# A three-block attention and MLP kernel: the low part of five weight blocks by GpSimd subtraction, and the third block's key, value and query rows interleaved

## The chip, the cores and the metric

The kernel runs on one core of a Trainium2 chip. The metric is the time of one execution on the device in microseconds (us), lower is better. PE is TensorE, ACT is ScalarE, DVE is VectorE, POOL is GpSimd and SP is SyncE, which only issues copies here.

## The reference

Two layers of one kind (l = 0 and 1 in the code) are followed by one of another kind (called 2). Between layers stands a layer norm, and ahead of the third block an RMS norm as well. All is float32.

```python
for l in range(DEPTH):                                   # DEPTH = 2
    proj = jnp.einsum('bld,de->ble', h, w_in[l])
    a, g, zc, q, k, v, za, qi, ki, wi = jnp.split(proj, IN_SPLITS, axis=-1)
    ...                                                  # convolution branch, sparse attention branch
    y = jnp.einsum('ble,ed->bld', jnp.concatenate([y_conv, y_attn], axis=-1), w_out[l])
    h = layer_norm(DEEPNORM_ALPHA * h + y, post_ln_g[l], post_ln_b[l])
x = h[:, N_META:L]
...
h = rmsnorm(x, norm_gain)                                # the third block
z = jnp.einsum('bsd,de->bse', h, w_in)
q, k, v, gate_a, u_in, v_in, gate_b, g_merge = jnp.split(z, IN_SPLITS_2, axis=-1)
q = axial_rope(rmsnorm(q, q_gain), row_ang, col_ang)
k = axial_rope(rmsnorm(k, k_gain), row_ang, col_ang)
```

The width is 1024, and there are 512 positions and 16 meta positions: row tile 0 has 16 rows, tiles 1 to 4 have 128 each.

## The kernel before

**Products in three passes.** PE multiplies with operands in a reduced format (fp32r). Each operand is split in a high part and the remainder, the low part, and a product is high x high, high x low and low x high (`PASSES`). `xhi` and `xlo` hold the turned rows of x: ACT writes `xhi` out of PSUM (`x_hi`, L807), DVE subtracts and writes `xlo` (`x_lo`, L1958). PE's products wait for `x_lo`.

**The weight stream.** Weights come in blocks of 128x2048 (1 MB) through a ring of four buffers. The list `USES` gives PE's order of products and `BLOCKS` the last use of each block. SP loads block n into `raw[n % 4]` when the last use of block n - 4 is done (L555). ACT then writes the high part `whi` (L631) and the negated high part `wlo`, which lies over the raw block (L632), both in `split_hi`. POOL then issues a copy that adds the weights from memory onto `wlo` (`split_lo`, L1050), so that raw - high is left. PE waits in `weights(n)` for that copy. `SPLIT_AT` says after which product a block is split; `next_blocks(use)` does it on ACT and on POOL. Only the first two blocks of the program get their low part from DVE.

**The borders.** Every engine runs its own list in order; nothing is scheduled at run time. At the end of a layer come, for the last row tiles, the two halves (convolution, attention) of the output products (`output_half`, L1428), then on DVE for each tile t `residual` (L1911, L1919), `aggregate` (L1924) and `post_norm` (L1934: h<-h,meanvar,post_ln_g; L1938: h<-h,rstd,post_ln_b), between the two on POOL `ln_deviation` (L1059 and L1062, which write `rstd`). PE turns the rows (`turn_rows`, L1412). Ahead of the third block ACT forms a sum of squares (`squares`, L817), POOL `input_deviation` and DVE `second_input` (L1950: h_normed<-h,rstd,norm_gain), before the rows are turned. The first products of layer 1 are those of a and g, over tiles 0 to 2 first and over tiles 3 and 4 after. The third block begins with kv (1 block, 256 columns) for its four row tiles, then q (2 blocks, 512 columns) for four, each product in bank A or B by turns (`rows`, L1279); a bank is free when ACT has taken its rows (L925, L928). SP issues `load_mix`, which waits for the last `post_norm`, right after q's second block.

## Time and profile before

| | us |
|---|---|
| median of 3 runs | 1060.81 |
| runs | 1059.41 to 1061.35 |
| profiled execution | 1061.86 |
| its span | 1060.1 |
| PE busy | 999.9 (94%) |
| DVE busy | 653.6 (62%) |
| ACT busy | 582.7 (55%) |
| POOL busy | 197.7 (19%) |

The span is the profiled execution from its first to its last instruction; 1.8 us lie around it. All times of rows are counted from the start of the span. The border between layers 0 and 1 lies at about 332 to 372 us, the one between layer 1 and the third block at 658 to 726 us. PE's matmuls are pipelined, so their busy time is not time at PE's peak; where PE stands still shows in the idle time ahead of an instruction. A releaser is inferred from semaphores, and where one instruction waits for several things the last by the profile is named.

### The profile page before, as it was taken

Reading aid. Unit: us, or ns where it says so; the run is one execution under the profiler, and the core shown is the slowest. Engines: PE = TensorE matmul, PEld = TensorE weight load, DVE = VectorE, ACT = ScalarE, POOL = GpSimd, SP = SyncE. Lnnn points to the kernel's source line nnn. Section 1 sums busy time; section 2 is a strip of 40 time slices with the busy share of each in tenths; the row PEclk is TensorE's granted clock in tenths of the full one; section 3 lists DMA queues with packets and bytes.
Section 4 is the critical chain, followed back from the end, with each engine's and each line's share of the span. In section 5 each row is a group of like instructions: output and inputs, shape, how many; then the busy total and the mean of one; then the engine's idle time right before and its main releaser. Section 6 shows DMA issues by size and latency. Waiting matters only on the chain.

```text
span 1060.1 us, 16512 instructions
## 1 busy us (share of the span) xinstructions
PE 999.9 (94%) x6452; PEld 845.2 (80%) x6452; DVE 653.6 (62%) x1423; ACT 582.7 (55%) x944; POOL 197.7 (19%) x238
## 2 busy tenths in 40 slices
PE   6999999898999899999999799789999899999997
PEld 6998988875577898898888577678888778887885
DVE  3899999866573489899977556626521433332522
ACT  6585882557444558587255734634555555554321
POOL 0000771013121100076101212223200000000001
PEclk9999999998999999999989999979999999999999
DMA  7776874734203777487464521765777545456651
GB/s 287 182 181 178 209 175 118 187 92 120 40 1 98 181 170 177 121 192 181 113 164 100 153 60 40 202 158 147 183 181 207 130 104 125 115 134 144 163 155 80
DMA packets 23820, 152.35 MB, mean 144 GB/s; under 512 B 2864, under 2 KB 3376, under 8 KB 6848
## 3 DMA queue, kind: packets, MB, share of 16 engines
q0 software_dynamic: 9648, 68.75, 34.8%
q1 hardware_dynamic: 14096, 82.55, 21.3%
q8 instruction: 52, 0.85, 0.3%
q14 instruction: 24, 0.20, 0.1%
HBM read 149.20 MB, written 2.10 MB: 143 GB/s over the span
## 4 chain that ended last, share of the span: by engine, by line
PE 61%; DVE 20%; ACT 9%; issue 7%; POOL 1%; DMA 1%; POOLq 0%; SPq 0%; DVEq 0%; ACTq 0%
PE psum_B L1246 15%; PE psum_A L1246 9%; PE psum_B L1279 7%; PE psum_A L1279 7%; DVE conv_acc L1723 6%; DVE score L1782 5%; PE psum_A L1428 5%; DVE top L1773 5%; PE psum_B L1428 2%; PE psum_A L1639 2%; PE psum_B L1382 2%; PE psum_B L1639 2%; ACT w_hi L631 2%; ACT w_lo L632 2%; PE psum_A L1357 1%
## 5 line engine op out<-in xcount | busy, mean ns | idle before, releaser
L1723 DVE SCALAR_TENSOR_TENSOR conv_acc<-u,vec,conv_acc 128x528 f32<-128x528 f32 (+1 forms) x240 | 172.1, 755 | 3.2
L1050 POOL DMA_DIRECT2D w_lo<-in_weights x67 | 59.4, 887 | 595.0 <-ACT w_lo L632 568.8
L1246 PE MATMUL psum_B<-x_hi,w_hi 128*128 128x264 f32 (+3 forms) x480 | 134.8, 321 | 5.2 <-DVE mlp_lo L2176 3.6
L631 ACT ACTIVATE w_hi<-w_raw 128x2048 fp32r<-128x2048 f32 (+2 forms) x85 | 129.3, 1521 | 15.0 <-DMA w_raw<-in_weights 14.5
L1246 PE MATMUL psum_B<-x_lo,w_hi 128*128 128x264 f32 (+3 forms) x480 | 132.5, 317 | 0.0
L1246 PE MATMUL psum_B<-x_hi,w_lo 128*128 128x264 f32 (+3 forms) x480 | 132.1, 316 | 0.0
L1246 PE MATMUL psum_A<-x_hi,w_hi 128*128 128x264 f32 (+2 forms) x528 | 127.3, 295 | 2.2 <-DVE za L1870 1.2
L632 ACT ACTIVATE w_lo<-w_raw 128x2048 fp32r<-128x2048 f32 (+2 forms) x85 | 128.6, 1513 | 0.0
L1246 PE MATMUL psum_A<-x_lo,w_hi 128*128 128x264 f32 (+2 forms) x528 | 124.6, 290 | 0.0
L1246 PE MATMUL psum_A<-x_hi,w_lo 128*128 128x264 f32 (+2 forms) x528 | 124.5, 290 | 0.0
L1246 PEld LDWEIGHTS psum_A<-x_hi,w_hi 128*128 128x128 f32 x528 | 89.4, 192 | 6.5 <-issue 3.3
L1246 PEld LDWEIGHTS psum_B<-x_hi,w_hi 128*128 128x128 f32 (+1 forms) x480 | 81.4, 185 | 13.7 <-issue 7.6
L1246 PEld LDWEIGHTS psum_A<-x_lo,w_hi 128*128 128x128 f32 x528 | 89.5, 192 | 0.8
L1246 PEld LDWEIGHTS psum_A<-x_hi,w_lo 128*128 128x128 f32 x528 | 89.3, 192 | 0.7
L1246 PEld LDWEIGHTS psum_B<-x_hi,w_lo 128*128 128x128 f32 (+1 forms) x480 | 81.4, 185 | 6.2
L1246 PEld LDWEIGHTS psum_B<-x_lo,w_hi 128*128 128x128 f32 (+1 forms) x480 | 81.4, 185 | 5.6
L1279 PE MATMUL psum_A<-w_hi,x_hi 128*128 128x512 f32 (+1 forms) x144 | 56.7, 394 | 4.9 <-DMA w_lo<-in_weights 2.6
L1279 PE MATMUL psum_B<-w_hi,x_hi 128*128 128x512 f32 (+1 forms) x144 | 56.5, 392 | 4.1 <-issue 4.1
L1782 DVE MATCH_REPLACE8 score<-top,score 128x528 f32<-128x528 f32 (+2 forms) x102 | 56.1, 561 | 0.0
L1279 PE MATMUL psum_B<-w_hi,x_lo 128*128 128x512 f32 (+1 forms) x144 | 55.9, 388 | 0.0
L1279 PE MATMUL psum_B<-w_lo,x_hi 128*128 128x512 f32 (+1 forms) x144 | 55.9, 388 | 0.0
L1279 PE MATMUL psum_A<-w_hi,x_lo 128*128 128x512 f32 (+1 forms) x144 | 55.7, 387 | 0.0
(349 smaller groups left out, 2121.9 us busy)
## 6 DMA issues: line engine op xcount, KB each, us to landing
w_raw<-in_weights SPq DMA_DIRECT2D x67, 1024.0 KB, 5.2
w_lo<-in_weights POOLq DMA_DIRECT2D x65, 1024.0 KB, 8.4
x_first<-in_x_t SPq DMA_DIRECT2D x4, 528.0 KB, 6.9
h<-in_x SPq DMA_DIRECT2D x1, 2048.0 KB, 10.8
out<-h SPq DMA_DIRECT2D x4, 512.0 KB, 2.6
post_ln_g<-in_post_ln_g SPq DMA_DIRECT2D x2, 512.0 KB, 6.9
post_ln_b<-in_post_ln_b SPq DMA_DIRECT2D x2, 512.0 KB, 7.9
w_raw<-in_weights SPq DMA_DIRECT2D x2, 288.0 KB, 5.3
```

The source lines that it names most:

```text
L631: act.activation(whi[n % RING][:, a:b], raw[n % RING][:, a:b], ACT.Copy)
L632: got = act.activation(wlo[n % RING][:, a:b], raw[n % RING][:, a:b], ACT.Copy, scale=-1.0)
L1050: pool.dma_start(wlo[n % RING][:, 0:width], io["weights"][n, :, 0:width], accum_op=ALU.add) \
L1246: mm = pe.matmul(ps[0:cols, i, 0:b - a], w[wp][:, kt, at:at + cols], x[xp][:, kt, a:b], start=(kt == 0 and wp + xp == 0), stop=(kt == KD - ...
L1279: mm = pe.matmul(ps[:, 0, 0:width], act_parts[xp][:, kt, c0:c0 + P], w[wp][:, kk, at:at + width], start=(kt == 0 and wp + xp == 0), stop=( ...
L1357: pe.transpose(main[:, 0, (j - 1) * P:(j - 1) * P + n], src[0:n, START[j]:END[j]], ident[0:n, 0:n])
L1382: mm = pe.matmul(ps[s:s + HD, 0, hd // 2 * P:hd // 2 * P + n], keys, probs, start=(j == 0), stop=(j == t))
L1428: mm = pe.matmul(ps, x[xp][:, kt, START[t]:START[t] + P], w[wp][:, kk, 0:DC], start=(kt == 0 and wp + xp == 0), stop=(kt == KD - 1 and wp ...
L1639: mm = pe.matmul(ps[:, 0, :], w[wp][:, kt, d % 4 * P:d % 4 * P + P], parts[xp][:, kt, :], start=(kt == 0 and wp + xp == 0), stop=(kt == CT ...
L1723: got = dve.scalar_tensor_tensor(dst, src, w, dst, ALU.mult, ALU.add)
L1773: dve.max(top8[:, t - 1, :], vals).then_inc(topk_max.mark((l, r, t)), 1)
L1782: dve.match_replace(vals, top8[:, t - 1, :], vals, MARK).then_inc(topk_marked.mark((l, r, t)), 1)
```

## The change

`LO_BY_POOL` names five blocks: a and g of layer 1, kv and the two of q. For these ACT writes the high part in two halves of 1024 columns and no negated copy, POOL subtracts high from raw for each half and writes `wlo` (`subtract_hi`), and PE waits for the second half's signal. No copy adds weights for them. In the third block PE's order becomes kv 0, kv 1, q 0, kv 2, kv 3, q 1, q 2, q 3 (`KV_AND_Q`), with the turn of tile 3 after kv 1 and that of tile 4 after q 0. In layer 1 the attention half of output tile (0, 4) goes ahead of that of (1, 3), DVE's residuals follow, and ACT's splits and squares are placed anew. SP issues `load_mix` one block later.

```diff
@@ -83,6 +83,9 @@
+KV_AND_Q = (("kv", 0), ("kv", 1), ("q", 0), ("kv", 2), ("kv", 3), ("q", 1), ("q", 2), ("q", 3))
 def weight_stream():
@@ -111,8 +114,11 @@
             uses.extend((l, "wo", n, t) for t in tiles if (n, t) < (1, 3) and t < 4)
-        uses.extend([(l, "wo", 0, 4, "conv"), (l, "wo", 1, 4, "conv"), (l, "wo", 1, 3, "conv"), (l, "wo", 1, 3),
-                     (l, "wo", 0, 4), (l, "wo", 1, 4)])
+        uses.extend([(l, "wo", 0, 4, "conv"), (l, "wo", 1, 4, "conv"), (l, "wo", 1, 3, "conv")])
+        if l < DEPTH - 1:
+            uses.extend([(l, "wo", 1, 3), (l, "wo", 0, 4), (l, "wo", 1, 4)])
+        else:
+            uses.extend([(l, "wo", 0, 4), (l, "wo", 1, 3), (l, "wo", 1, 4)])
@@ -143,8 +149,9 @@
     blocks.append(((l, "kv", 0), BLOCK, (l, "kv", 3)))
-    uses.extend((l, "kv", t) for t in range(4))
-    halves(l, "q", range(4))
+    for half in range(2):
+        blocks.append(((l, "q", half), BLOCK, (l, "q", 3)))
+    uses.extend((l, *row) for row in KV_AND_Q)
     for name in ("vin", "u", "gb"):
@@ -161,6 +168,8 @@
 NUMBER = {key: n for n, (key, _, _) in enumerate(BLOCKS)}
+LO_BY_POOL = {NUMBER[key] for key in ((1, "a", 0), (1, "g", 0), (2, "kv", 0), (2, "q", 0), (2, "q", 1))}
@@ -609,7 +619,7 @@
                 load_weights(n)
-                if key == (2, "q", 1):
+                if key == (2, "vin", 0):
                     load_mix()
@@ -627,6 +637,12 @@
                     act.activation(whi[n][:, a:b], raw[n][:, a:b], ACT.Copy).then_inc(hi_made.mark(("w", n)), 1)
+                    return
+                if n in LO_BY_POOL:
+                    for half in range(2):
+                        a, b = half * BLOCK // 2, (half + 1) * BLOCK // 2
+                        act.activation(whi[n % RING][:, a:b], raw[n % RING][:, a:b], ACT.Copy) \
+                            .then_inc(hi_made.mark(("w", n, half)), 1)
                     return
@@ -909,13 +925,10 @@
                     x_hi(l, 1)
+                    next_blocks((l, "wo", 0, 4))
                     x_hi(l, 2)
+                    next_blocks((l, "wo", 1, 3))
                     squares(3, square)
-                    next_blocks((l, "wo", 1, 3))
-                    x_hi(l, 3)
-                    squares(4, square)
-                    next_blocks((l, "wo", 1, 4))
-                    x_hi(l, 4)
@@ -933,7 +946,6 @@
                     act.activation(sgb[t][:, :], ps[:, 0, :], ACT.Silu).then_inc(act_took.mark(use), 1)
-                next_blocks(use)
@@ -996,12 +1008,20 @@
-            for name in ("kv", "q"):
-                for t in range(4):
-                    take_rows(name, t)
+            for name, t in KV_AND_Q:
+                take_rows(name, t)
+                if (name, t) == ("kv", 1):
+                    x_hi(DEPTH - 1, 3)
+                    squares(4, square)
+                elif (name, t) == ("q", 0):
+                    x_hi(DEPTH - 1, 4)
+                    split_hi(NUMBER[(2, "vin", 0)])
+                elif name == "q":
+                    next_blocks((2, "q", t))
             for name in ("vin", "u", "gb"):
                 for t in range(4):
                     take_rows(name, t)
+                    next_blocks((2, name, t))
                     if name == "u":
@@ -1043,6 +1063,13 @@
         def _(pool):
+            def subtract_hi(n, half):
+                a, b = half * BLOCK // 2, (half + 1) * BLOCK // 2
+                pool.wait_ge(hi_made.sem, hi_made.at(("w", n, half)))
+                pool.tensor_tensor(wlo[n % RING][:, a:b], raw[n % RING][:, a:b], whi[n % RING][:, a:b].bitcast(F32),
+                                   ALU.subtract).then_inc(pool_lo.mark((n, half)), 1)
             def split_lo(n):
@@ -1154,15 +1181,27 @@
-                next_blocks((l, "wo", 1, 4, "conv"))
-                ln_deviation((l, "post", 3), 3, P)
-                if l == DEPTH - 1:
+                if l < DEPTH - 1:
+                    a_in, g_in = NUMBER[(1, "a", 0)], NUMBER[(1, "g", 0)]
+                    subtract_hi(a_in, 0)
+                    subtract_hi(a_in, 1)
+                    ln_deviation((l, "post", 3), 3, P)
+                    subtract_hi(g_in, 0)
+                    subtract_hi(g_in, 1)
+                    ln_deviation((l, "post", 4), 4, P)
+                    next_blocks((l, "wo", 1, 4))
+                else:
+                    kv_in, q_in = NUMBER[(2, "kv", 0)], NUMBER[(2, "q", 0)]
+                    subtract_hi(kv_in, 0)
+                    subtract_hi(kv_in, 1)
+                    subtract_hi(q_in, 0)
+                    ln_deviation((l, "post", 3), 3, P)
+                    subtract_hi(q_in, 1)
                     input_deviation(3)
-                next_blocks((l, "wo", 1, 3))
-                ln_deviation((l, "post", 4), 4, P)
-                if l == DEPTH - 1:
+                    subtract_hi(q_in + 1, 0)
+                    ln_deviation((l, "post", 4), 4, P)
+                    subtract_hi(q_in + 1, 1)
                     input_deviation(4)
-                next_blocks((l, "wo", 1, 4))
@@ -1174,11 +1213,11 @@
+            split_lo(NUMBER[(2, "vin", 0)])
             for t in range(4):
-                next_blocks((2, "kv", t))
                 unit_scale("k", t)
+            next_blocks((2, "q", 1))
             for t in range(4):
-                next_blocks((2, "q", t))
                 unit_scale("q", t)
@@ -1223,8 +1262,11 @@
                     pe.wait_ge(first_lo.sem, first_lo.at(n))
+                elif n in LO_BY_POOL:
+                    pe.wait_ge(pool_lo.sem, pool_lo.at((n, 1)))
                 elif n:
-                    pe.wait_ge(weights_lo[n % RING], 16 * (n // RING + (n % RING >= BY_DVE)))
+                    added = [m for m in range(n % RING, n + 1, RING) if m >= BY_DVE and m not in LO_BY_POOL]
+                    pe.wait_ge(weights_lo[n % RING], 16 * len(added))
                 return whi[n % RING], wlo[n % RING]
@@ -1548,13 +1590,17 @@
                 output_conv(l, 1)
-                if l == DEPTH - 1:
-                    turn_rows(l, 1)
-                output_rows(l, 1, 3, "A", 0)
                 if l < DEPTH - 1:
+                    output_rows(l, 1, 3, "A", 0)
                     turn_rows(l, 0)
                     turn_rows(l, 1)
-                output_attn(l, 0)
+                    output_attn(l, 0)
+                else:
+                    turn_rows(l, 1)
+                    ps = claim((l, "wo", 1, 3), "A", (0,))[:, 0, :]
+                    output_half(l, 1, 0, 3, ps).then_inc(psum_full.mark((l, "wo", 1, 3, "conv")), 1)
+                    output_attn(l, 0)
+                    output_half(l, 1, 1, 3, ps).then_inc(psum_full.mark((l, "wo", 1, 3)), 1)
                 turn_rows(l, 2)
@@ -1640,13 +1686,16 @@
-            for t in range(4):
-                x_ready(1, t + 1)
-                rows((2, "kv", t), NUMBER[(2, "kv", 0)], x, META + P * t, 1, 2 * P, 0, KD)
-                if t < 2:
-                    turn_rows(1, t + 3)
-            for t in range(4):
-                rows((2, "q", t), NUMBER[(2, "q", 0)], x, META + P * t, 2)
+            for name, t in KV_AND_Q:
+                if name == "kv":
+                    x_ready(1, t + 1)
+                    rows((2, "kv", t), NUMBER[(2, "kv", 0)], x, META + P * t, 1, 2 * P, 0, KD)
+                    if t == 1:
+                        turn_rows(1, 3)
+                else:
+                    rows((2, "q", t), NUMBER[(2, "q", 0)], x, META + P * t, 2)
+                    if t == 0:
+                        turn_rows(1, 4)
             for name in ("vin", "u", "gb"):
@@ -2048,13 +2097,13 @@
                     x_lo(l, 1)
+                    residual(l, 0, 4)
                     residual(l, 1, 3)
                     aggregate(l, 3)
                     post_norm(l, 3)
-                    residual(l, 0, 4)
                     x_lo(l, 2)
+                    residual(l, 1, 4)
                     second_input(3)
-                    residual(l, 1, 4)
                     aggregate(l, 4)
                     post_norm(l, 4)
                     x_lo(l, 3)
```

The order of POOL's instructions at the border to the third block, before (w_lo_59 is kv's block, w_lo_60 and w_lo_57 are q's, w_lo_58 is vin's first):

```order
163 L1070 TENSOR_TENSOR x_lo<-y_part_125,x_hi 128x4x128
164 L1050 DMA w_lo_59<-in_weights 128x2048
165 L1059 TENSOR_SCALAR var_eps<-meanvar 128x1
166 L1062 TENSOR_TENSOR rstd<-var_eps,minus_half 128x1
167 L1059 TENSOR_SCALAR var_eps<-prob_sums 128x1
168 L1062 TENSOR_TENSOR rstd<-var_eps,minus_half 128x1
169 L1050 DMA w_lo_60<-in_weights 128x2048
170 L1059 TENSOR_SCALAR var_eps<-meanvar 128x1
171 L1062 TENSOR_TENSOR rstd<-var_eps,minus_half 128x1
```

The same place on POOL now (L1070 is the subtraction in `subtract_hi`):

```order
164 L1070 TENSOR_TENSOR w_lo_59<-w_raw_55,w_hi_51 128x1024 x2
165 L1070 TENSOR_TENSOR w_lo_60<-w_raw_56,w_hi_52 128x1024
166 L1086 TENSOR_SCALAR var_eps<-meanvar 128x1
167 L1089 TENSOR_TENSOR rstd<-var_eps,minus_half 128x1
168 L1070 TENSOR_TENSOR w_lo_60<-w_raw_56,w_hi_52 128x1024
169 L1086 TENSOR_SCALAR var_eps<-prob_sums 128x1
170 L1089 TENSOR_TENSOR rstd<-var_eps,minus_half 128x1
171 L1070 TENSOR_TENSOR w_lo_57<-w_raw_53,w_hi_49 128x1024
172 L1086 TENSOR_SCALAR var_eps<-meanvar 128x1
173 L1089 TENSOR_TENSOR rstd<-var_eps,minus_half 128x1
174 L1070 TENSOR_TENSOR w_lo_57<-w_raw_53,w_hi_49 128x1024
```

Subtractions now stand ahead of and between the deviations of tiles 3 and 4 (var_eps, rstd), where issues of copies stood.

POOL at the border between layers 0 and 1 before, with the waits (w_lo_58 is a's block, w_lo_59 g's):

```order
86 L1050 DMA w_lo_58<-in_weights 128x2048 [waits weights_minus]
87 L1059 TENSOR_SCALAR var_eps<-meanvar 128x1 [waits stats_made]
88 L1062 TENSOR_TENSOR rstd<-var_eps,minus_half 128x1 [waits pool_step]
89 L1050 DMA w_lo_59<-in_weights 128x2048 [waits weights_minus]
90 L1059 TENSOR_SCALAR var_eps<-meanvar 128x1 [waits stats_made]
```

And now:

```order
86 L1070 TENSOR_TENSOR w_lo_58<-w_raw_54,w_hi_50 128x1024 [waits hi_made] x2
87 L1086 TENSOR_SCALAR var_eps<-meanvar 128x1 [waits stats_made]
88 L1089 TENSOR_TENSOR rstd<-var_eps,minus_half 128x1 [waits pool_step]
89 L1070 TENSOR_TENSOR w_lo_59<-w_raw_55,w_hi_51 128x1024 [waits hi_made] x2
90 L1086 TENSOR_SCALAR var_eps<-meanvar 128x1 [waits stats_made]
```

The two halves of each block take the place of one issue; DVE's order at this border is what it was.

ACT at the border to the third block now, from the first split on (w_hi_51 is kv's block, w_hi_52 and w_hi_49 q's, w_hi_50 vin's):

```order
510 L644 ACTIVATE w_hi_51<-w_raw_55 128x1024 [waits raw_loaded2]
511 L644 ACTIVATE w_hi_51<-w_raw_55 128x1024
512 L823 ACTIVATE x_hi<-psum_D 128x8x128 [waits psum_full]
513 L644 ACTIVATE w_hi_52<-w_raw_56 128x1024 [waits raw_loaded3]
514 L644 ACTIVATE w_hi_52<-w_raw_56 128x1024
515 L823 ACTIVATE x_hi<-psum_C 128x8x128 [waits psum_full]
516 L644 ACTIVATE w_hi_49<-w_raw_53 128x1024 [waits raw_loaded0]
517 L644 ACTIVATE w_hi_49<-w_raw_53 128x1024
518 L833 ACTIVATE square,prob_sums<-h 128x1024 [waits exp_made,normed]
519 L941 ACTIVATE qk_row_173<-psum_A 128x128 [waits psum_full]
```

Both of q's blocks are split ahead of the square of tile 3; before, the first followed that square, and the second that of tile 4.

## Rows read from the trace of the kernel before

**Rows 1.** Chain that ended last, border to third block: start, length, what.
```profile
688.92 5.04 PE psum_A L1279 x24
693.97 4.10 issue
698.07 5.46 PE psum_B L1279 x24
...
720.28 5.56 PE psum_B L1279 x24
```

**Rows 2.** Timeline of PE there: start, length, instruction, idle before and releaser.
```profile
674.21 0.40 PE L1428 MATMUL psum_B<-w_lo,x_hi 128*128 128x512 f32 x1
677.18 0.36 PE L1279 MATMUL psum_A<-w_hi,x_hi 128*128 128x256 f32 x1 [2.58 <-DMA w_lo<-in_weights]
...
680.11 1.03 PE L1412 MATMUL psum_D<-ident,h_normed 128*128 128x128 f32 x8
680.90 0.36 PE L1279 MATMUL psum_B<-w_hi,x_hi 128*128 128x256 f32 x1
```

**Rows 3.** Busy time by window: PE, PEld, DVE, ACT, POOL, clock, DMA, GB/s.
```profile
690.00:710.00 20.00, 15.90 (x74) 14.49 (x74) 3.89 (x19) 5.62 (x10) 4.42 (x9) 0.75 0.77 186
```

**Rows 4.** Timeline of PE at the border of layers 0 and 1.
```profile
349.74 0.36 PE L1246 MATMUL psum_A<-x_hi,w_hi 128*128 128x264 f32 x1 [1.05 <-DVE x_lo L1958]
...
359.97 0.36 PE L1246 MATMUL psum_D<-x_hi,w_hi 128*128 128x264 f32 x1 [2.40 <-DVE x_lo L1958]
```

**Rows 5.** Landing of copies issued at 347.3 (w_lo), 665.4 and 683.7 (w_raw).
```profile
DMA to landing us min/median/max: 12.6/12.6/12.6
...
DMA to landing us min/median/max: 6.0/6.0/6.0
...
DMA to landing us min/median/max: 10.2/10.2/10.2
```

**Rows 6.** The page's part 6: issues, KB each, median us to landing.
```profile
w_raw<-in_weights SPq DMA_DIRECT2D x67, 1024.0 KB, 5.2
w_lo<-in_weights POOLq DMA_DIRECT2D x65, 1024.0 KB, 8.4
```

**Rows 7.** Timeline of ACT: high parts at both borders.
```profile
343.21 1.91 ACT L631 ACTIVATE w_hi<-w_raw 128x2048 fp32r<-128x2048 f32 x1
...
662.21 1.92 ACT L631 ACTIVATE w_hi<-w_raw 128x2048 fp32r<-128x2048 f32 x1 [2.01 <-DMA w_raw<-in_weights]
...
693.93 1.91 ACT L631 ACTIVATE w_hi<-w_raw 128x2048 fp32r<-128x2048 f32 x1 [5.11 <-DMA w_raw<-in_weights]
```

**Rows 8.** POOL's subtractions by shape (count, busy us, mean ns); then min/median/max ns.
```profile
L1070 POOL TENSOR_TENSOR x_lo<-y_part,x_hi 128x64 fp32r<-128x64 f32 x2 | 0.6, 317 | 6.7 <-ACT x_hi L777 6.7
...
L1070 POOL TENSOR_TENSOR x_lo<-y_part,x_hi x18: 314/1282/1597, 224.5 to 660.3; 128x512 fp32r<-128x512 f32 x16, 128x64 fp32r<-128x64 f32 x2
```

**Rows 9.** Timeline of POOL beside DVE, and durations of DVE's L1950.
```profile
660.27 1.60 POOL L1070 TENSOR_TENSOR x_lo<-y_part,x_hi 128x512 fp32r<-128x512 f32 x1 [11.82 <-ACT x_hi L777]
...
669.96 1.27 POOL L1059 TENSOR_SCALAR var_eps<-meanvar 128x1 f32<-128x1 f32 x1 [2.77 <-DVE meanvar L1924]
...
674.54 0.19 POOL L1059 TENSOR_SCALAR var_eps<-prob_sums 128x1 f32<-128x1 f32 x1 [2.66 <-ACT square L817]
...
L1950 DVE SCALAR_TENSOR_TENSOR h_normed<-h,rstd,norm_gain x4: 1276/1282/2312, 659.4 to 684.5; 128x1024 f32<-128x1024 f32 x4
```

**Rows 10.** Timeline of DVE at both borders.
```profile
344.49 1.27 DVE L1934 SCALAR_TENSOR_TENSOR h<-h,meanvar,post_ln_g 128x1024 f32<-128x1024 f32 x1
345.80 1.28 DVE L1938 SCALAR_TENSOR_TENSOR h<-h,rstd,post_ln_b 128x1024 f32<-128x1024 f32 x1
...
348.33 1.21 DVE L1958 TENSOR_TENSOR x_lo<-psum_C,x_hi 128x1024 fp32r<-128x1024 f32 x1
...
669.90 1.28 DVE L1934 SCALAR_TENSOR_TENSOR h<-h,meanvar,post_ln_g 128x1024 f32<-128x1024 f32 x1
...
674.51 1.21 DVE L1958 TENSOR_TENSOR x_lo<-psum_C,x_hi 128x1024 fp32r<-128x1024 f32 x1
```

More of the change, by code:

```diff
@@ L501, in build @@
         first_lo = signal("first_lo")
+        pool_lo = signal("pool_lo")
         psum_full = signal("psum_full")
```

## The prediction

> **What bounds the kernel now.** I read the page first: TensorE (PE) is busy 94% of the span, so a change pays only where PE stands still or runs at a low clock. Next I read the chain of waits around the two places that the diff touches. At the border between the second and third block the chain shows the kv product of tile 2 taking 5.04 us, then 4.10 us of idle, then that of tile 3 taking 5.46 us [rows 1]. PE also waited 2.58 us for the low part of kv; the product of kv 0 then took 2.93 us, from 677.18 to the turn at 680.11 [rows 2]. From 690 to 710 the granted clock is 0.75 while PE is busy 15.90 of 20 us [rows 3]. So this border loses at least 6.7 us in idle time (2.58 + 4.10) and 4.6 us in clock (5.04 + 5.46 less 2 x 2.93). At the border between the first and second block PE loses only 1.05 us (for x_lo of tile 2) and 2.40 us [rows 4]. The latter is put down to x_lo, but the g block's low part, issued at 347.3, took 12.6 us to land [rows 5], which is 359.83, 0.14 us before PE goes on. That product reads tiles 0 to 2 alone, so the transfer held it.
>
> **Low part by subtraction.** Removed for five blocks: ACT's second 1.9 us pass, a GpSimd issue of 0.9 us and an accumulating transfer of 8.4 us median [rows 6]. Added: per block two 128x1024 subtractions. 128x512 took 1.28 us (the median) and 128x64 0.32 us [rows 8]; the line through them gives 2.38 us for 1024 columns (0.32 + 960 x 2.15 ns), and doubling the first 2.56. No row shows this form, so the bounds are 2.3 and 2.6 and I take 2.4, the line's value. ACT's half pass is 0.95 us, half of 1.90 [rows 7]. So a low part is ready 0.95 + 4.8 = 5.8 us after ACT starts, where before it took 3.6 + 8.4 us or more.
>
> The Trainium skill (GPSIMD Engine Reference, 3.1 Elementwise) gives 4497 ns for a fp32 subtraction-like operation of 2048 columns; as an estimate that is 2.25 us for 1024 and would make the gain some 0.6 us larger. No row of this trace has that width.
>
> **What the subtraction does to VectorE.** The gain is not free. When GpSimd's 128x512 subtraction began waiting at 660.27 it took 1.60 instead of 1.28, and the VectorE operation h_normed<-h,gain that came behind it took 2.31 us, where the others of its kind took 1.28 [rows 9]. The other way round var_eps took 1.27 us at 669.96, all of it beside h<-h,ln_g, but 0.19 us beside x_lo<-psum,x_hi [rows 9, 10]. I read: a VectorE operation with two SBUF inputs and a GpSimd operation exclude each other, and whichever has begun keeps the other out until about its end; one with a PSUM input is free. A 2.4 us subtraction can then hold back a post_norm (two such operations) by 2.2 to 2.4 us each time, and post_norm stands ahead of x_lo, which PE needs.
>
> The Trainium skill (SBUF — State Buffer, section SBUF: two separate sides) calls this "an exclusive lock, not a bandwidth split", kept for the whole instruction. It speaks against this change; the rows show it for 1.3 us operations alone. With that rule the sum is the one below; if long operations shared instead, it would be the third rival.
>
> **First border, step by step.** a's low part is ready at 335.8 + 0.95 + 4.8 = 341.6 instead of 348.8, but PE waits for x_lo of tile 2 (VectorE 348.33 + 1.21 [rows 10]), so nothing is gained. g: ACT's first half ends at 343.21 + 0.95 = 344.2 [rows 7], GpSimd runs 344.3 to 346.7. VectorE wants h<-h,ln_g at 344.49 [rows 10]: it gets 346.5 to 347.8. GpSimd's second half has waited and goes before VectorE's dependent second operation: 347.8 to 350.2. VectorE's h<-h,rstd,ln_b then starts at 350.0 instead of 345.80, so x_lo of tile 2 starts at 348.33 + 4.2, and PE begins the a product at 353.9 instead of 349.74: 4.2 us lost. PE has stood 5.4 us by then. After 4.10 us of standing the product took 5.46 instead of 2.9; I put 1.5 us on the clock here, between 0 and 2.5. The 2.40 us wait for g's transfer goes. What is late next there is x_lo of tiles 3 and 4, 2.3 us behind the turn of tile 4, covered by the g product of 2.9 us. Sum: 4.2 + 1.5 - 2.4 = **3.3 us lost**. If VectorE gets h<-h,ln_g in first (0.2 us decides), one subtraction less stands in the way: about 2.2 us lost, less a clock that stays high: near 0. Ends: 4.5 lost, 2.4 won.
>
> The second layer between the borders has the same order and waits as before, so it moves as one; PE's two spells of low clock in it may fall otherwise, worth 1.5 us either way.
>
> **Second border.** PE's queue: attention half of (0,4) ahead of that of (1,3), which lets q's second block load 2.8 us earlier; kv 0, kv 1, turn 3, q 0, turn 4, kv 2, kv 3, q 1 to 3. SP loads vin's first block right when its buffer is free (674.6) and not behind load_mix, which waits for the last post_norm; that load started at 683.7 and landed 10.2 us later [rows 5], and ACT stood 5.11 us for it at 693.93 [rows 7] with kv 1's rows, which PE waited for, behind it. This is the 4.10 us. Times of before, carried through the new queues:
> - kv: raw at 662.2 [rows 7], both low halves at 668.1. PE starts kv 0 right after the last output product, which began at 674.21 [rows 2]: 674.4 instead of 677.18.
> - q's first block: issued at 665.41, landed after 6.0 us before [rows 5] with the kv transfer beside it; alone 5.2 [rows 6], so 670.6. ACT's first half 671.6, GpSimd 671.6 to 674.0. ln_deviation of tile 3, for which statistics are there at 672.6, is queued behind it. h<-h,ln_g 673.9 to 675.1; ln_deviation 675.1 to 675.9; then GpSimd goes straight into the next subtraction, 675.9 to 678.3, and h<-h,rstd,ln_b waits again: 678.2 to 679.5. x_lo of tile 2 is ready at 680.7, so kv 1 starts at 680.9, where it started before [rows 2]. The 2.8 us won by kv 0 are lost, and PE has stood 3.5 us, so I let kv 1 take 5.2 us at low clock: 686.1, turn 3: 687.0.
> - q 0, two halves of 2.8: 687.0 to 692.8. q's second block is subtracted at 681.6 to 684.0 and 687.4 to 689.8, in time for the second half at 690.
> - The second subtraction holds the second operation of tile 4's post_norm until 689.7; square, input_deviation and second_input follow to 694.3. Turn 4 begins at 694.5 (PE stands 1.7), kv 2 at 695.3, kv 3 at 698.2, q 1 at 701.2, each q row 5.56 us: q 3 ends at 717.8 instead of 725.8 [rows 1]. **8.0 us won.** The waits for ACT are gone, since kv 1's rows are taken at 686.4 and vin's split stands behind tile 4.
> - vin's second block is split after q 1 (707.4 to 711.0), its transfer lands 8.4 us after (719.5 to 721); PE wants it at 720.6. I put 0.2 us; 1.2 at the far end.
>
> Ends for this border: VectorE favoured in each contest 8 to 9 won; subtraction of 2.6 us 7.3; raw landings as before (6.0 and 7.9) 7.2. From q 3 on all orders are as before.
>
> **Sum.** 3.3 - 8.0 + 0.2 = -4.5 us. The profiled execution took 1061.86 us (span 1060.1 and 1.8 around it), so 1057.4 in its terms; it stands 1.05 above the median of the three runs, 1060.81, from which I forecast **1056.3 us**. A comparison of this kernel can tell about 0.2%, 2.1 us, from no change.
>
> **Rivals.**
> 1. VectorE gets in ahead of GpSimd at the borders (0.18). For it: at the first border 0.2 us decides, and after a GpSimd operation VectorE has been the one waiting. Against: at 660.7 GpSimd, having waited, went before VectorE's next. First border 0, second 8.2 to 9: 1052.2.
> 2. Slower: the 128x1024 subtraction takes much longer than its line says (0.12). GpSimd's queue is then the bound: four subtractions stand in the chain of the second border and two at the first, and every ln_deviation is behind one. Each microsecond more costs about 4.2 and up to 2 us. At 3.15 us a half nothing is won; at 3.6 us it is 1063.5. Against it: 16 operations of 512 columns took 1.28 us in the middle and 1.60 at most [rows 8], also while ACT and the DMA engines work. Raw blocks landing 5 us late, as vin's did [rows 5], would have the same effect on a smaller scale.
> 3. The long subtraction does not hold VectorE back (0.05): first border 2.4 won; at the second PE never stands and q 3 ends at 674.4 + 4 x 2.93 + 4 x 5.56 + 1.6 for the turns and 1.2 for short waits, 711.2, so 14.6 won: 1044.0. Against: rows 9.
> 4. The gain is as reckoned at one border and lost to clock or a late vin transfer (0.17): within 2.1 us of before, 1059.5.
> The forecast as reckoned, 1054 to 1058.5, has 0.48.
>
> **Range and chances.** 1050.5 to 1060.5 holds the forecast, most of rival 1 and much of rival 4. Faster by over 0.2%: 0.48 + 0.18 + 0.05 = 0.71; within: 0.17; slower: 0.12.
>
> **What would show it.** In the profile after: GpSimd's 128x1024 subtractions at 2.4 us; h<-h,ln_g and h<-h,rstd,ln_b at 344 to 351 and 673 to 680 taking up to 3.5 us instead of 1.28, or starting late; PE's a product near 353.9 and no wait for g; kv 0 straight after the output products, kv 1 no earlier than before; no ACT wait for w_raw at 694; q 3 ending about 4.5 us earlier by the profile's clock, since the first border's loss is carried along. It would be wrong if the first border gains, or if kv 1 starts before 680.9 plus the first border's shift.

## The result, and the profile after

The changed kernel is slower: 1064.93 us median of 4 runs beside 1060.11 for the kernel before on the same chip, ratio 1.0048 (95% interval 1.0030 to 1.0067). A second comparison, below, gave 1.0034 (1.0017 to 1.0051). I had forecast 1056.3 us. The profiled execution has a span of 1063.0 us (1060.1 before); PE, DVE and POOL are busy 1000.8, 663.9 and 218.1 us.

**First border.** Timelines of POOL and then of DVE in the changed kernel: start, length, instruction (L1070 is the subtraction).

```profile
338.65 4.74 POOL L1070 TENSOR_TENSOR w_lo<-w_raw,w_hi 128x1024 fp32r<-128x1024 f32 x2 [1.96 <-ACT w_hi L644]
346.10 5.70 POOL L1070 TENSOR_TENSOR w_lo<-w_raw,w_hi 128x1024 fp32r<-128x1024 f32 x2 [1.10 <-ACT w_hi L644]
...
346.25 3.32 DVE L1983 SCALAR_TENSOR_TENSOR h<-h,meanvar,post_ln_g 128x1024 f32<-128x1024 f32 x1
349.61 3.27 DVE L1987 SCALAR_TENSOR_TENSOR h<-h,rstd,post_ln_b 128x1024 f32<-128x1024 f32 x1
```

The two DVE operations took 1.27 and 1.28 us before [rows 10]. They are stretched by 2.0 us each, beside g's two subtractions. PE's timeline and the chain show what follows (before: [rows 4]):

```profile
355.54 0.56 PE L1288 MATMUL psum_A<-x_hi,w_hi 128*128 128x264 f32 x1 [5.08 <-DVE x_lo L2007]
...
355.54 5.62 PE psum_A L1288 x24
361.15 0.88 PE psum_D L1454 x8
362.04 2.90 PE psum_B L1288 x24
```

PE stands 5.08 us, not 1.05, and the first product after it takes 5.62 us, the next 2.90 (it took 3.15 us before). The granted clock is 0.66 from 354 to 364.

**Second border.** The timelines of POOL and PE:

```profile
677.12 2.42 POOL L1070 TENSOR_TENSOR w_lo<-w_raw,w_hi 128x1024 fp32r<-128x1024 f32 x1 [3.35 <-ACT w_hi L644]
...
686.71 0.55 PE L1321 MATMUL psum_B<-w_hi,x_hi 128*128 128x256 f32 x1 [3.60 <-DVE h L1960]
...
699.53 1.06 PE L1454 MATMUL psum_C<-ident,h_normed 128*128 128x128 f32 x8 [0.88 <-DVE h_normed L1999]
```

So far it went as the steps said. The chain behind that had no place in them. It runs from kv 2 to vin's first row tile:

```profile
700.60 2.85 PE psum_B L1321 x24
703.44 2.85 PE psum_A L1321 x24
706.32 10.50 DMA w_raw<-in_weights
716.84 1.92 ACT w_hi L647
718.75 1.81 ACT w_lo L648
720.57 0.43 issue
721.00 8.82 DMA w_lo<-in_weights
729.82 0.04 issue
729.87 4.52 PE psum_A L1321 x12
```

kv 3 ends at 706.3 and frees the buffer for vin's second block; its copy takes 10.5 us, the split 3.7, the accumulating transfer 8.8. PE has done the q rows and half of vin's first row tile by then, stands 4.13 us, and does the other half at a low clock, 4.52 us instead of 2.78 (half of a row's 5.56); the granted clock is 0.72 from 729 to 735. PE's timeline, the first matmul of the late half:

```profile
729.87 0.79 PE L1321 MATMUL psum_A<-w_hi,x_hi 128*128 128x512 f32 x1 [4.13 <-DMA w_lo<-in_weights]
```

**How stretches are compared.** Single times can't be set side by side, because the executions differ before the first border already: the layer's last y_part starts at 332.21 in the profile of before and 333.97 in that of after. I therefore measure each border from that layer's own last y_part. These are the four rows for the changed kernel (DVE's y_part, u and y_part, then ACT's first v_normed):

```profile
333.97 0.69 DVE L1937 SCALAR_TENSOR_TENSOR y_part<-psum_B,za 128x512 f32<-128x512 f32 x1 [5.80 <-PE psum_B L1424]
376.45 0.71 DVE L1755 SCALAR_TENSOR_TENSOR u<-shifted,u 128x528 f32<-128x528 f32 x1 [8.32 <-ACT shifted L691]
664.50 0.69 DVE L1937 SCALAR_TENSOR_TENSOR y_part<-psum_B,za 128x512 f32<-128x512 f32 x1 [5.80 <-PE psum_B L1424]
734.43 0.60 ACT L944 ACTIVATE v_normed<-psum_A 128x512 f32<-128x512 f32 x1 [9.54 <-PE psum_A L1321]
```

Their differences are border 1 (42.5), the layer between, and border 2 (69.9). "To a" is from y_part to PE's first a product, "vin to end" from that v_normed to the end of the span. The same instructions give, in every profile of this study:

| kernel | to a | border 1 | between | border 2 | vin to end |
|---|---|---|---|---|---|
| before, four profiles | 17.5 all | 38.6, 37.9, 38.0, 38.6 | 288.0, 287.9, 288.3, 288.1 | 72.6, 68.7, 69.5, 72.6 | 328.6 all |
| changed, two profiles | 21.6 both | 42.5, 42.5 | 288.0, 288.1 | 69.9, 71.5 | 328.6, 329.0 |
| first border undone, two | 17.5 both | 38.9, 39.0 | 287.9, 288.1 | 69.8, 69.8 | 328.6 both |
| first border alone | 21.6 | 42.6 | 288.1 | 72.5 | 328.6 |
| vin subtracted | 21.6 | 42.6 | 288.1 | 64.1 | 328.6 |
| vin's first block only | 21.6 | 42.8 | 288.0 | 64.1 | 328.6 |
| vin's second block only | 21.6 | 42.5 | 288.1 | 64.0 | 328.5 |
| pieces of 512 columns | 19.4 | 39.4 | 288.0 | 69.4 | 328.6 |
| undone, vin subtracted | 17.5 | 42.0 | 288.3 | 64.1 | 328.6 |
| 512, vin subtracted | 19.4 | 39.4 | 286.3 | 62.3 | 328.7 |
| 256, vin subtracted, two | 18.3 both | 36.8, 38.3 | 286.8, 288.0 | 64.8, 63.5 | 328.6, 328.7 |
| 512, vin subtracted, plain order | 19.4 | 39.4 | 286.7 | 70.8 | 328.6 |

The last column says that nothing comes back later (one profile of the changed kernel is 0.4 us longer there): what a border wins or loses stays.

### The profile page after: what moved, and what is told of

Read it like the earlier page. It is cut to its first block, busy times and chain, and to the rows that moved or that the text cites. A ratio compares the mean times of both kernels' runs of the same rounds, so it can differ in the third digit from the quotient of the medians.

```text
span 1063.0 us, 16517 instructions
## 1 busy us (share of the span) xinstructions
PE 1000.8 (94%) x6452; PEld 846.8 (80%) x6452; DVE 663.9 (62%) x1423; ACT 574.3 (54%) x944; POOL 218.1 (21%) x243
## 4 chain that ended last, share of the span: by engine, by line
PE 58%; DVE 21%; ACT 9%; issue 7%; DMA 3%; POOL 1%; POOLq 0%; DVEq 0%; SPq 0%; ACTq 0%
PE psum_B L1288 15%; PE psum_A L1288 9%; DVE conv_acc L1772 6%; PE psum_B L1321 5%; PE psum_A L1321 5%; DVE score L1831 5%; DVE top L1822 5%; PE psum_A L1470 5%; PE psum_B L1470 2%; PE psum_A L1685 2%; DMA w_raw<-in_weights 2%; PE psum_B L1685 2%; PE psum_B L1424 2%; ACT w_hi L647 2%; ACT w_lo L648 2%
## 5 line engine op out<-in xcount | busy, mean ns | idle before, releaser
L1077 POOL DMA_DIRECT2D w_lo<-in_weights x62 | 54.8, 884 | 579.5 <-ACT w_lo L648 553.3
L647 ACT ACTIVATE w_hi<-w_raw 128x2048 fp32r<-128x2048 f32 (+2 forms) x80 | 119.8, 1497 | 10.0 <-DMA w_raw<-in_weights 9.4
L648 ACT ACTIVATE w_lo<-w_raw 128x2048 fp32r<-128x2048 f32 (+2 forms) x80 | 119.1, 1489 | 0.0
## 6 DMA issues: line engine op xcount, KB each, us to landing
w_raw<-in_weights SPq DMA_DIRECT2D x2, 288.0 KB, 5.4
```

The source lines that it names most:

```text
L647: act.activation(whi[n % RING][:, a:b], raw[n % RING][:, a:b], ACT.Copy)
L648: got = act.activation(wlo[n % RING][:, a:b], raw[n % RING][:, a:b], ACT.Copy, scale=-1.0)
L1077: pool.dma_start(wlo[n % RING][:, 0:width], io["weights"][n, :, 0:width], accum_op=ALU.add) \
```

## Experiments

**Which border loses.** Two kernels take the change apart. In the first, a and g get their low parts by transfer again:

```diff
-LO_BY_POOL = {NUMBER[key] for key in ((1, "a", 0), (1, "g", 0), (2, "kv", 0), (2, "q", 0), (2, "q", 1))}
+LO_BY_POOL = {NUMBER[key] for key in ((2, "kv", 0), (2, "q", 0), (2, "q", 1))}
...
                 if l < DEPTH - 1:
-                    a_in, g_in = NUMBER[(1, "a", 0)], NUMBER[(1, "g", 0)]
-                    subtract_hi(a_in, 0)
-                    subtract_hi(a_in, 1)
+                    next_blocks((l, "wo", 1, 4, "conv"))
                     ln_deviation((l, "post", 3), 3, P)
-                    subtract_hi(g_in, 0)
-                    subtract_hi(g_in, 1)
+                    next_blocks((l, "wo", 1, 3))
```

> The changed kernel with the border between the two layers as before: the low parts of the a and g blocks come again by the accumulating transfer. Theory A (the loss has two places): in the profile after, the first border ends 3.9 us later than before (374.6 against 369.0, less the 1.8 us by which that execution lay behind already), and the second wins only 2.7. With the first undone the time falls by about 4 us from the changed kernel, to 0.996 to 0.998 of the kernel before. Theory B (the first border's loss is of that one execution, and the rest of the change costs time): it stays at 1.003 to 1.005 of the kernel before. Theory C (both borders lose): 1.001 to 1.003.

The second is the kernel before with only these two blocks subtracted (the same edit the other way round, on the kernel before).

> The kernel before with only the low parts of a and g at the border between the layers by GpSimd subtraction; the third block is as before. Theory A: 3.9 us slower, 1.003 to 1.005; the two DVE passes of the post-norm at 346 to 353 take 3.3 us each instead of 1.3, and the first product after the border runs at the lower clock. Theory B: 0.999 to 1.001. The two halves of the change should add up: this ratio and that of the kernel with the first border undone should make that of the whole change when multiplied.

Measured: 1.0006 (0.9990 to 1.0023) and 1.0038 (1.0017 to 1.0060). Their product is 1.0044, so the halves add up to the whole. The first border's loss is real and is the whole loss: border 1 takes 42.6 us with it and 38.9 without. But my own theory missed 0.996 to 0.998 for the first: by its stretches the second half of the change wins 2.8 us against the first profile of before, and no such gain is in its time. That was open until the profiles of before were repeated (below).

**Why vin is late.** Both vin blocks are subtracted too:

```diff
-LO_BY_POOL = {..., (2, "q", 0), (2, "q", 1))}
+LO_BY_POOL = {..., (2, "q", 0), (2, "q", 1), (2, "vin", 0), (2, "vin", 1))}
...
+            def low_part(n):
+                if n in LO_BY_POOL:
+                    subtract_hi(n, 0)
+                    subtract_hi(n, 1)
+                else:
+                    split_lo(n)
+
             def next_blocks(use):
                 for n in SPLIT_AT.get(use, []):
-                    split_lo(n)
+                    low_part(n)
...
-            split_lo(NUMBER[(2, "vin", 0)])
+            low_part(NUMBER[(2, "vin", 0)])
```

> The changed kernel, with both vin blocks' low parts by GpSimd subtraction too. Theory A says that the second border gives back 6 us at vin, since its second block's copy lands 10.5 us after its issue beside the first block's accumulating transfer, and its own accumulating transfer takes 8.8 more. Both transfers are gone here: TensorE's idle 6.5 us between the halves of vin's row tile 0 goes, and the time falls by 5 to 7 us from the changed kernel, to 0.998 to 0.9995. Rival: the copy lands as late and the ScalarE rows of q delay the split, so that TensorE waits as long: 1.004 to 1.005. A second rival: the subtractions hold GpSimd from the scales of k and q and VectorE's passes on them, so that part comes back later in the third block: 1.001 to 1.003.

Measured 0.9970 (0.9954 to 0.9986), which is lower than I expected; border 2 takes 64.1 us instead of 69.9. Its chain has nothing but PE left, from kv 3 through the q rows to vin 0:

```profile
703.97 2.84 PE psum_A L1328 x24
706.81 5.55 PE psum_B L1328 x24
712.36 5.56 PE psum_A L1328 x24
717.92 5.56 PE psum_B L1328 x24
723.48 5.56 PE psum_A L1328 x24
```

Two more kernels subtract one vin block each (only the set in the first two lines differs). Both have one profile each and no ratio of their own, so the stretches speak for them.

> The changed kernel with only vin's first block by subtraction; its second keeps the accumulating transfer. If the second block's copy is late because it runs beside the first block's accumulating transfer, the copy now lands about 5 us after kv 3's end instead of 10.5 (in the kernel with both subtracted it did), the split starts right after q 1, its transfer lands near 725, and TensorE waits at most 1 us in vin's row tile 0: second stretch 64 to 65.5 us instead of 69.9. Rival (the copy is late for another reason, and the accumulating transfer of the second block is what costs): the copy lands after 9 to 10 us, second stretch 68 to 70 us.

> The changed kernel with only vin's second block by subtraction; the first keeps the accumulating transfer. The second block's copy should land late again, 10 to 11 us after kv 3's end, since the transfer is beside it; the two hi halves and subtractions take 6 us from there, so that the low part is there about 723, 3 us before TensorE wants it: no wait, second stretch 64 to 64.6 us, as with both subtracted. If GpSimd's scales of k and q come in between, up to 66.

Landing of vin's second raw block, issued at kv 3's end, in the changed kernel, with vin's first block subtracted, and with only the second:

```profile
DMA to landing us min/median/max: 10.5/10.5/10.5
...
DMA to landing us min/median/max: 5.0/5.0/5.0
...
DMA to landing us min/median/max: 10.3/10.3/10.3
```

So the copy takes twice as long when the first block's accumulating transfer, issued 0.7 us before it, is under way. Issued 0.9 us ahead of such a transfer, a copy landed after 6.0 us [rows 5]. Border 2 takes 64.1 and 64.0 us: taking away either the collision or the last transfer removes the whole wait. It needs both a late copy and 8.8 us of transfer behind it.

**What DVE waits for.** Every subtraction is cut into pieces of 512 columns, with the semaphore on the last:

```diff
-                pool.tensor_tensor(wlo[n % RING][:, a:b], raw[n % RING][:, a:b], whi[n % RING][:, a:b].bitcast(F32),
-                                   ALU.subtract).then_inc(pool_lo.mark((n, half)), 1)
+                for c in range(a, b, 512):
+                    got = pool.tensor_tensor(wlo[n % RING][:, c:c + 512], raw[n % RING][:, c:c + 512],
+                                             whi[n % RING][:, c:c + 512].bitcast(F32), ALU.subtract)
+                got.then_inc(pool_lo.mark((n, half)), 1)
```

> The changed kernel with every subtraction in pieces of 512 columns rather than 1024. If a DVE pass with two SBUF inputs waits for the GpSimd operation that is under way (an exclusive lock held for one operation), its wait falls from up to 2.4 us to up to 1.2: the two post-norm passes of the first border take 2.0 to 2.8 us rather than 3.3, and the time falls by 1 to 2 us, to 1.002 to 1.004 of the kernel before. If the slowdown is one of shared bandwidth, the piece's size changes nothing: passes of 3.3 us, 1.004 to 1.005. If the lock is won by GpSimd again at each piece, DVE waits longer than now: over 1.005.

Measured 0.9986 (0.9969 to 1.0002): 6.6 and 5.1 us under the changed kernel by its two ratios, where its stretches say 3.6 (3.1 at border 1, 0.5 at border 2) and I had expected 1 to 2. The passes of 2.2 us are those of the first hypothesis; the time lies below all three. DVE's two post-norm operations of the first border, with pieces of 512, and then of 256 columns in a later kernel (vin subtracted there as well):

```profile
343.91 2.22 DVE L1985 SCALAR_TENSOR_TENSOR h<-h,meanvar,post_ln_g 128x1024 f32<-128x1024 f32 x1
346.17 2.20 DVE L1989 SCALAR_TENSOR_TENSOR h<-h,rstd,post_ln_b 128x1024 f32<-128x1024 f32 x1
...
346.56 1.68 DVE L1992 SCALAR_TENSOR_TENSOR h<-h,meanvar,post_ln_g 128x1024 f32<-128x1024 f32 x1
348.27 1.64 DVE L1996 SCALAR_TENSOR_TENSOR h<-h,rstd,post_ln_b 128x1024 f32<-128x1024 f32 x1
```

And the subtractions' durations (ns, min/median/max) with 1024, 512 and 256 columns (all ten of the first kernel, those of the first border in the others):

```profile
L1070 POOL TENSOR_TENSOR w_lo<-w_raw,w_hi x10: 2379/2398/3346, 338.7 to 692.3; 128x1024 fp32r<-128x1024 f32 x10
...
L1071 POOL TENSOR_TENSOR w_lo<-w_raw,w_hi x8: 1256/1290/2273, 336.2 to 349.5; 128x512 fp32r<-128x512 f32 x8
...
L1071 POOL TENSOR_TENSOR w_lo<-w_raw,w_hi x16: 718/730/1730, 338.9 to 353.2; 128x256 fp32r<-128x256 f32 x16
```

These DVE operations, with two SBUF inputs, are stretched by 2.0, 0.9 and 0.4 us where the GpSimd operation takes 2.4, 1.3 and 0.7: each time by one GpSimd operation less 0.3 to 0.4 us. PE's a product moves by just twice that (4.0, 1.9 and 0.8 us). The first border also pays less clock: the a product took 5.62 us with 1024 columns and 4.44 with 512, where PE stands 2.9 us ahead of it instead of 5.1.

> As the kernel with pieces of 512 and vin by subtraction, but pieces of 256 columns. If DVE waits for one GpSimd operation at each pass, the two post-norm passes of the first border take 1.6 to 2.0 us (2.2 with 512, 3.3 with 1024, 1.28 alone), the subtraction of a half costs about 0.3 us more in all, and the first border takes 38.8 to 39.3 us. If the wait is not one operation's but a share of the time, it stays at 2.2.

> Pieces of 256 columns with vin by subtraction, timed. In the profile its first border took 36.8 us (39.4 with pieces of 512, 42.5 with 1024, 38.6 and 37.9 before) and its second 64.8 (62.3 with 512, with the clock higher there). So 2.6 us less at the first and 2.5 more at the second: 0.992 to 0.994, the same as with 512. If the second border's difference is clock of the execution alone, 0.990 to 0.992.

The durations came out as expected. The first border did not: it took 36.8 us and, in the second profile, 38.3, where I had put 38.8 to 39.3. PE stands 1.8 us in both, and the a product behind takes 3.19 us in one and 4.43 in the other. The time, 0.9938 (0.9919 to 0.9956), is that of the kernel with 512: the last microsecond at border 1 is too small to tell.

**Both mended.**

> The first border as before (accumulating transfers for a and g) together with both vin blocks' low parts by GpSimd subtraction. The theory adds stretches: the border between the layers costs 0.3 us against the kernel before (last y_part to the first use of the new u), the second border to vin's first row tile takes 64.1 us as in the kernel with vin subtracted, against 72.6 before. So 8.2 us under the kernel before, 0.991 to 0.994. Rival (the clock takes back what the shorter waits give, in stretches that the profiled execution doesn't show): 0.995 to 0.999, though the stretches are as said.

> The whole change with all subtractions in pieces of 512 columns, and vin's two blocks by subtraction too. By stretches: the first border 39.4 us (38.6 before), the second 63.5 to 64.1 (72.6 before), so 7.5 to 8.3 us under the kernel before: 0.992 to 0.995, equal to the kernel with the first border undone and vin subtracted within 0.1%. If small pieces gain more than DVE's shorter waits explain, it is below that one. Rival as there: 0.995 to 0.999.

Measured 0.9934 (0.9909 to 0.9960) and 0.9929 (0.9908 to 0.9949), 1053.3 and 1052.2 us against 1060.05: both beat both kernels, and are equal to each other, as said. A miss is the first border of the former, 42.0 us where I had put 38.9. There the g product waits for its transfer again, 3.10 us, and then runs at the lower clock (PE's timeline, then the chain):

```profile
360.18 0.56 PE L1292 MATMUL psum_D<-x_hi,w_hi 128*128 128x264 f32 x1 [3.10 <-DMA w_lo<-in_weights]
...
360.18 5.62 PE psum_D L1292 x24
```

In the two profiles of the kernel with the first border undone and vin as it was, the wait was 2.7 us, and the product took 3.14 and 3.15 us.

**What the new order is worth.** In the kernel with pieces of 512 and vin subtracted, the third block's rows are put back in plain order, kv 0 to 3 and then q 0 to 3. The turn of tile 4 and its x_hi then stand behind kv 2, and the split that would move to q 0 is kept behind q 1; of the edit, the list alone is shown:

```diff
-KV_AND_Q = (("kv", 0), ("kv", 1), ("q", 0), ("kv", 2), ("kv", 3), ("q", 1), ("q", 2), ("q", 3))
+KV_AND_Q = (("kv", 0), ("kv", 1), ("kv", 2), ("kv", 3), ("q", 0), ("q", 1), ("q", 2), ("q", 3))
```

> All low parts of the five blocks and of vin by subtraction in pieces of 512 columns, and the third block's rows in plain order: kv 0 to 3, then q 0 to 3. If the gain of the second border comes from the interleaving (TensorE has q 0 to do while it waits for the third and fourth tile's norm), this one is 4 to 6 us slower than the same kernel with rows interleaved, at 0.997 to 0.999 of before. If it comes from the low part of kv and q that no longer waits for a transfer, it stays at 0.993 to 0.994: kv 1 is late either way, and the order only moves the wait.

Measured 0.9989 (0.9969 to 1.0009), against 0.9929 interleaved; border 2 takes 70.8 us against 62.3. PE waits 3.4 and 2.4 us for x_lo of tiles 3 and 4 with nothing to do, and its kv products take 4.29 and 4.64 us; the interleaved kernel does kv 2 and 3 in 2.84 each (chains of both):

```profile
688.73 4.29 PE psum_A L1331 x24
...
696.62 4.64 PE psum_B L1331 x24
...
694.06 2.84 PE psum_B L1330 x24
696.90 2.84 PE psum_A L1330 x24
```

So without the interleaving, the subtractions (and the later `load_mix`, which this kernel keeps) gain nothing that can be told. That they are what allows q 0 to stand between kv 1 and kv 2 is argued, not shown: no kernel has the new order with the transfers. In the first profile of before, the low parts of q's two blocks landed 28.1 and 38.7 us after y_part, and the interleaved kernel starts the two halves of q 0 at 26.7 and 30.4.

**How steady the stretches are.** The kernels as they were, once more each:

> The changed kernel again, for a second profile of it and a ratio on the same chip as the others. By the stretches of its first profile it is 1.2 us slower than before (3.9 lost at the first border, 2.7 won at the second): 1.001. By its first timing it is 1.0048. The stretches should repeat within 0.3 us (42.5 at the first border, 69.9 at the second); where the last y_part of the first layer ends (332.2 or 334.0 in the profiles so far) should vary, if that is the clock of the execution and not the change.

> The kernel before once more, for a second profile. The kernel with only the second border changed is by its stretches 2.4 us under before, yet its time was 1.0006 of it; so either the first profile of before has a long stretch by its clock (then here the second border takes about 70 us instead of 72.6, and the second half of the change wins nothing), or the changed kernels have bad clocks outside their profiles (then the second border takes 72.3 to 72.7 again).

> The kernel before, a third profile. Stretch from the last y_part of the second layer to vin's first row tile: 72.6 us if its first profile and that of the kernel with only the first border changed (72.5) are the usual case, with a granted clock of 0.5 to 0.8 between 25 and 45 us behind that y_part; 68.7 if the second profile is.

> The same, a fourth profile: 68.7 to 69.5 us or 72.5. If it is something else again, the stretch depends on the execution in more than two ways, and single profiles can't price a change of 3 us there.

> The kernel with the first border undone, a second profile. In its first the second border took 69.8 us. 69.5 to 70 again says that the changed order is steady there; 71.5 as in the second profile of the whole change says that its clock varies as well, and the half wins nothing on average (its time was 1.0006 of before).

The change again gave 1.0034; its stretches repeat but for 1.5 us at border 2, where the late transfer took 9.45 us, not 8.82, and vin's late half 5.49, not 4.52. For the kernel before, border 2 takes 72.6, 68.7, 69.5 and 72.6 us, and 72.5 in the kernel with the first border alone. The difference lies in the stretch that I priced from [rows 1]. In the second profile, and then in the fourth, the chain reads:

```profile
691.67 3.08 PE psum_A L1279 x24
694.74 3.07 issue
697.81 3.08 PE psum_B L1279 x24
...
688.72 3.08 PE psum_A L1279 x24
691.80 6.43 issue
698.24 5.46 PE psum_B L1279 x24
```

Not the clock alone differs. The five executions with the old order at this border, times of row tiles and waits in us:

| profile | wait before kv 0 | kv 0 | vin's copy lands after | kv 3 starts, from y_part | PE idle before it | kv 3 | border 2 |
|---|---|---|---|---|---|---|---|
| before, first | 2.6 | 3.1 | 10.2 | 39.2 | 4.1 | 5.46 | 72.6 |
| before, second | 3.2 | 4.6 | 8.5 | 37.8 | 3.1 | 3.08 | 68.7 |
| before, third | 3.8 | 5.5 | 9.0 | 38.5 | 0 | 2.94 | 69.5 |
| before, fourth | 2.9 | 3.1 | 9.8 | 39.3 | 6.4 | 5.46 | 72.6 |
| first border alone | 2.7 | 3.1 | 9.9 | 39.0 | 3.9 | 5.46 | 72.5 |

In the two short ones kv's transfer lands later, kv 0 runs at a lower clock, and ACT and POOL come to q's second block 2 to 3.5 us later. Its accumulating transfer then starts later beside vin's copy, which is issued at the same time (25 us after y_part) in all five, and the copy lands earlier. kv 3, which waits for it by way of ACT, starts up to 1.5 us earlier (in the third profile right behind kv 2, which took 5.46 us) and runs at the high clock, about 2.4 us less. So a late transfer at one place makes the border shorter as a whole. That the shorter overlap is what lets the copy land earlier is read from the order of events; the experiments on vin show the same kind of collision by an edit. The half of the change that remains when the first border is undone is steady, 69.8 us in both profiles. So it wins 2.8 us against some executions of before and loses 1.1 against others; against the mean of the five, 71.2, it wins 1.4, of which border 1 takes back 0.7 (39.0 against the mean of 38.3). That leaves 0.7 us, within the interval of its time, 1.0006 (0.9990 to 1.0023): no difference that can be told.

## Why the prediction was wrong, point by point

- **Subtraction 2.4 us:** right (2.40 median).
- **The exclusion of DVE and GpSimd:** right, also for long operations, and DVE did not get in first (rival 1) nor share (rival 3). The Trainium skill (SBUF — State Buffer, SBUF: two separate sides) has the lock held for the whole instruction; with that rule the stretches for the three piece lengths agree, 2.0, 0.9 and 0.4 us. What I did not ask is whether shorter pieces would shorten the wait, which follows from the rule.
- **First border, 3.3 lost:** mechanism right, size a little small. The a product starts 4.0 us later (4.2 said), the clock costs 2.5 (5.62 less 3.1; 1.5 said), g's wait is gone. 3.9 lost against the first profile of before, 4.3 between the means of all profiles (42.6 and 38.3).
- **Second border, 8.0 won up to q 3:** right against the profile that it was worked out from. In it q 3 is taken 67.0 us after y_part (725.87 less 658.84), in the changed kernel 58.5 (722.99 less 664.50): 8.5 won. kv 1 still waits 3.6 us, as said.
- **Vin's second block, 0.2 us: this step failed.** It cost 5.9 us (734.43 against q 3's 722.99 + 5.56). The prediction has the split right behind q 1 and no term for the copy that it needs: it took it as landed by then. But the new order also puts vin's first split, and with it an accumulating transfer, at kv 3's end, when the second block's buffer comes free. The copy then takes 10.5 us, the split begins at 716.8 instead of 711.9 behind q 1, and the transfer lands at 729.8, 4.1 us after PE wants it; the clock falls meanwhile. My own [rows 5] showed a copy of 10.2 us in the kernel before; I let it bear on a rival and not on this term, whose far end I put at 1.2. With it at its size the forecast would have been near -4.5 + 5.7 = 1.2 us slower: within 0.2%. The path was right, but it had no term for the copy: the accumulating transfer itself took 8.8 us, near the 8.4 said.
- **The base.** Another 1.4 us come from the 72.6 us that the border takes in the profile that I worked from. It contains kv 3 at the lower clock, 5.46 us, and 4.1 us of idle; the mean of five executions is 71.2. I took one execution for the usual case, and two of the five lose 3 to 4 us less there.
- **From means:** border 1 +4.3 and border 2 -0.9 (70.25 over the four profiles with the new order, vin as it was and pieces of 1024, against 71.17) make +3.4 us, 1.0032. The two comparisons gave 1.0034 and 1.0048. The difference to the latter is within its interval. In the terms of the sum: -4.5, with 5.7 more for vin's copy, 1.4 for the base, 1.0 for the first border and 0.5 less up to q 3, is +3.1.
- **Rivals.** The late vin transfer was named in rival 4, with a chance of 0.17 and a time of 1059.5: right in kind, wrong in size and on the wrong side. The slower rival that I gave, a long subtraction, didn't occur. The sentence that all orders are as before from q 3 on was true and beside the point: the order was the same, but not the time between a buffer's release and its use.

## What to carry to other kernels

When a change lets PE run earlier, follow each ring buffer behind it one round further: from its last reader through copy, split and second transfer to the next use, with durations for transfers that overlap, not the median. Where a GpSimd operation may run beside VectorE operations with two SBUF inputs on the critical path, cut it short; the delay is that of one piece. And take the base of a sum from more than one execution where PE stands still, since the clock behind such a stand, and the landing of transfers beside each other, differ between executions of the same kernel.

## What the runs showed of the hardware

- A 1 MB copy of 5.0 us takes 10.3 to 10.5 us when an accumulating transfer of the same size starts 0.7 us ahead of it; both then land within 0.5 us of each other (at about 716.3 and 716.8). In the kernel before, a copy issued 0.9 us ahead of the transfer (at 665.4) took 6.0 us, and the transfer 10.8.
- The same kernel gets its low clock in another place from one execution to the next. With pieces of 256, PE stands 1.81 and 1.80 us before the a product, 18.3 us after y_part in both, and the product takes 3.19 us in one and 4.43 in the other. After 3.07 us of standing, kv 3 took 3.08 us in the kernel before; after 3.10 us, g took 5.62 in the kernel with the first border undone and vin subtracted. The stretch between the borders is 1.2 to 1.7 us shorter than usual in three of the 18 profiles, while "to a" repeats within 0.1 us.
- A GpSimd subtraction costs about 0.2 us for each further piece (two of 1.29 for one of 2.40, four of 0.73), little beside what the shorter hold gives back.
